# Block products in the second block's input projection, and a convolution split over three engines

## The reference

```python
u = h @ w_in_l                        # h: 512 x 1024, w_in_l: 1024 x 2048
ka, va = jnp.split(hc @ w_in_l[:, OFF_AK:OFF_BQ], 2, axis=-1)   # the 256 context tokens
...
def conformer_conv(u, conv_w, conv_b, ln_g, ln_b):
    a, gate = jnp.split(u, 2, axis=-1)
    h = a * jax.nn.sigmoid(gate)
    h = lax.conv_general_dilated(h, conv_w[:, None, :], window_strides=(1,), padding=((half, half),),
                                 feature_group_count=C_CHANNELS) + conv_b       # 31 taps, 256 channels
    return jax.nn.silu(layer_norm(h, ln_g, ln_b))
```

## Time and profile before

| what | value |
|---|---|
| median of 3 runs | 2835.19 us (2834.72 to 2843.73) |
| the profiled execution | 2836.13 us |
| span of its profile | 2834.3 us |
| mean granted clock of TensorE | 0.983 of full speed |
| `project2` in layer 0, first to last matmul | 974.85 to 1150.70 us |
| `project2` in layer 1 | 2004.33 to 2143.30 us |

### The profile page before, as it was taken

The page is one execution under the profiler, slowest core; times in us unless marked ns, Lnnn a source line. Parts: engine busy times, 40 slices in busy tenths (PEclk is TensorE's granted clock), DMA queues, the critical chain, the costliest instruction groups (busy, mean ns, idle before and its releaser), DMA issues. The chain is left out here.

```text
span 2834.3 us, 36392 instructions
## 1 busy us (share of the span) xinstructions
PE 2712.9 (96%) x15414; PEld 1568.9 (55%) x15414; DVE 1091.4 (39%) x2334; ACT 600.5 (21%) x1265; POOL 63.6 (2%) x61
## 2 busy tenths in 40 slices
PE   8998989999999999999799999999999989999998
PEld 7786755688864556764533333333777554444442
DVE  3523454477730365675620001113556560111212
ACT  4212234201110201562400000001215331001002
POOL 0000000000000000000001111110000000000000
PEclk9999999999999999999899999999999999999999
DMA  4228781222221211000489999996210038999995
GB/s 159 70 90 293 274 322 38 89 89 90 78 103 45 117 55 50 16 16 28 191 335 399 403 398 401 389 393 285 72 60 16 16 145 342 422 422 422 422 422 235
DMA packets 87478, 582.02 MB, mean 205 GB/s; under 512 B 10186, under 2 KB 11754, under 8 KB 21780
## 3 DMA queue, kind: packets, MB, share of 16 engines
q1 hardware_dynamic: 78244, 554.66, 49.3%
q0 software_dynamic: 6544, 21.24, 2.5%
q10 hardware_dynamic: 2528, 3.80, 0.4%
HBM read 561.96 MB, written 17.70 MB: 205 GB/s over the span
## 5 line engine op out<-in xcount | busy, mean ns | idle before, releaser
L3043 PE MATMUL ps<-ring,xsL 128*64 128x512 f32 x1320 | 298.2, 604 | 5.7 <-ACTq L217 5.7
L3043 PEld LDWEIGHTS ps<-ring,xsL 128*64 128x64 f32 x1320 | 96.2, 139 | 200.9 <-issue 194.9
L3301 DVE TENSOR_TENSOR hidL<-hidL,ps 128x1024 f32<-128x1024 f32 x16 | 19.5, 1221 | 473.6 <-PE ps L3043 473.6
L2618 PE MATMUL ps<-both,ring 128*128 128x384 f32 x480 | 158.0, 491 | 1.9 <-PEq L1834 1.9
L1841 PE MATMUL ps<-ring,actT 128*128 128x512 f32 x352 | 151.6, 592 | 1.1 <-PEq L2034 1.1
L3043 PE MATMUL ps<-ring,htL 128*64 128x512 f32 x640 | 143.9, 600 | 3.4 <-ACTq L217 3.2
L865 PE MATMUL ps<-both,ring 128*128 128x264 f32 x640 | 143.8, 386 | 1.4 <-PEq L642 1.4
L865 PEld LDWEIGHTS ps<-both,ring 128*128 128x128 f32 x640 | 121.4, 190 | 22.9 <-issue 2.3
L3331 ACT ACTIVATE hidL<-ps 128x1024 f32<-128x1024 f32 x16 | 16.4, 1024 | 541.7 <-PE ps L3051 303.4
L2618 PEld LDWEIGHTS ps<-both,ring 128*128 128x128 f32 x480 | 91.8, 192 | 66.5 <-issue 5.5
L2618 PE MATMUL ps<-tokens_b,ring 128*128 128x256 f32 (+1 forms) x480 | 121.9, 415 | 2.3 <-PEq L2223 2.3
(11 more groups left out here) (571 smaller groups left out, 3973.8 us busy)
## 6 DMA issues: line engine op xcount, KB each, us to landing
ring<-in_w_exp SPq DMA_DIRECT2D x245, 1024.0 KB, 13.7
ring<-in_w SPq DMA_DIRECT2D x73, 1024.0 KB, 5.0
tokens_b<-in_w_exp SPq DMA_DIRECT2D x63, 1024.0 KB, 13.8
ring<-in_w_mod SPq DMA_DIRECT2D x48, 1024.0 KB, 5.3
h<-in_w_exp SPq DMA_DIRECT2D x37, 1024.0 KB, 17.5
lent<-in_w_exp SPq DMA_DIRECT2D x26, 1024.0 KB, 15.9
both<-in_w_exp SPq DMA_DIRECT2D x13, 1024.0 KB, 18.6
gb<-in_rows SPq DMA_DIRECT2D x8, 512.0 KB
```

The lines of the kernel that those rows point to most:

```text
L2618: mm = pe.matmul(ps[:, bank + h, 0:half], w(c_), uT[:, c_, h * half:(h + 1) * half], start=c_ == 0, stop=c_ == KD - 1, skip_group_check=True)
L3043: mm = pe.matmul(ps[HD * par:HD * par + HD, bank + half, :], lhsL(kk, par), weights(kk)[:, half, par, :], start=kk == 0, stop=kk == KD - 1 ...
L3301: dve.tensor_tensor(h[:, :], h[:, :], src, ALU.mult).then_inc(hid.sem, 1)
```

## The change

Each chunk of weights becomes one 2 x 2 block product: the two halves of the input channels by the two tiles of columns on one side, by the two halves of the tokens on the other. It is made of seven block products in place of eight. A product has four matmuls of 128 x 128 weights by `H` tokens, 384 in layer 0 and 256 in layer 1. They go to four PSUM banks in the order P1, P7, P2 (on top of P1), P6, P5, P4, P3 (on top of P5). VectorE forms four sums of the token blocks once (`t1` to `t4`) and four sums of weight blocks per chunk (`s1` to `s4`), always for the next chunk, and combines the products in five sums per chunk. ScalarE copies P1 and later P1 + P2, and then scales or reorders the tiles (`finish_tiles`). In layer 1 the context's keys and values are made by plain products at the end of chunks KA, VB and KB (`context`). The values of the first attention come out with channels on the partitions like all others and are transposed afterwards (`turn_va`).

The convolution is split by group. Group 0 stays on VectorE, with its taps placed between the sums. For group 1 ScalarE writes each scaled, shifted tap into one of two buffers, and GpSimd adds it to `z`; `turn_z` waits for both groups. ScalarE takes over the copy of `vb` from VectorE, and the sums for the bias are split in two.

The eight sums need room: four of the ring's slots serve as scratch while `project2` runs. `slot_order` therefore gives the eight input chunks only four slots and puts the output projection's chunks into the scratch slots, and `limit` keeps their loads back until `project2` is over.

```diff
-            k.stream.limit = len(k.stream.chunks)
+            k.stream.limit = k.moe_at[0] - N_OUT2
...
+            stream.limit = k.moe_at[l + 1] - N_OUT2 if not last else len(stream.chunks)
...
+    K2, H = KD // 2, nq // 2
+    CIN, GATE, QA, QA2, KA, QB, VB, KB = range(N_IN2)
...
+    room_of = [k.stream.ring[:, x, :] for x in k.scratch[l]]
+    t1, t2, t3, t4 = (x[:, 0:K2 * H].rearrange("p (k t) -> p k t", k=K2) for x in room_of)
+    s1, s2, s3, s4 = (x[:, K2 * H:K2 * H + K2 * P].rearrange("p (k c) -> p k c", k=K2) for x in room_of)
+    b11, b12, b21, b22 = (uT[:, K2 * kh:K2 * kh + K2, h * H:(h + 1) * H] for kh in range(2) for h in range(2))
...
+            def product(out, w, x, start=True):
+                for c_ in range(K2):
+                    mm = pe.matmul(out, w[:, c_, :], x[:, c_, :], start=start and c_ == 0, stop=c_ == K2 - 1, skip_group_check=True)
+                mm.then_inc(ready.sem, 1)
...
+            def turn_va():
+                pe.wait_ge(assembled.sem, assembled.of(4 * KA + 3))
+                if kv:
+                    pe.wait_ge(ctx_read.sem, ctx_read.of(1))
+                for t in range(NT2):
+                    mm = pe.transpose(at_va[:, P * t:P * t + P], plain[1][:, P * t:P * t + P], c("ident"))
+                mm.then_inc(a_turned.sem, 1)
...
-                pe.wait_ge(filtered.sem, filtered.of(1))
+                pe.wait_ge(filtered.sem, filtered.of(2))
+                pe.wait_ge(a_taken.sem, a_taken.of(1))
...
-                project(i)
+            for i in range(N_IN2):
+                stream.wait(pe, chunk[i])
+                if i:
+                    pe.wait_ge(copied.sem, copied.of(2 * i))
+                product(bank(0), block_of(i, 0, 0), b11)
+                if i == QB:
+                    turn_va()
+                elif i == KB:
+                    rotate(3)
+                pe.wait_ge(weight_sums.sem, weight_sums.of(3 * i + 1))
+                if i:
+                    pe.wait_ge(assembled.sem, assembled.of(4 * i - 1))
+                product(bank(1), s3, t3)
+                pe.wait_ge(copied.sem, copied.of(2 * i + 1))
+                product(bank(0), block_of(i, 0, 1), b21, start=False)
+                if i == VB:
+                    turn_z()
+                pe.wait_ge(weight_sums.sem, weight_sums.of(3 * i + 2))
+                if i - 1 in kv:
+                    pe.wait_ge(ctx_read.sem, ctx_read.of(sum(x < i for x in kv)))
+                product(bank(2), s2, t2)
+                if i == VB:
+                    rotate(2)
+                elif i == KB:
+                    rotate(4)
+                    turn_values()
+                if i:
+                    pe.wait_ge(assembled.sem, assembled.of(4 * i))
+                product(bank(3), s1, t1)
+                if i == VB:
+                    turn_back()
+                pe.wait_ge(weight_sums.sem, weight_sums.of(3 * i + 3))
+                pe.wait_ge(assembled.sem, assembled.of(4 * i + 1))
+                product(bank(1), block_of(i, 1, 1), t4)
+                if i == QB:
+                    rotate(1)
+                pe.wait_ge(assembled.sem, assembled.of(4 * i + 2))
+                product(bank(3), s4, b22, start=False)
+                if i in kv:
+                    context(i)
+                stream.freed(chunk[i], ready.sem, ready.of(at(i, CONTEXT if i in kv else P4)))
...
+            def finish_tiles(i):
+                for j in (1, 0):
+                    act.wait_ge(assembled.sem, assembled.of(4 * i + 4 - j))
+                    x = tiles[i][j]
+                    if i == GATE:
+                        steps.free(act.activation(x[:, 0:nq], x[:, 0:nq], ACT.Sigmoid))
+                    elif i in (QA, QA2):
+                        steps.free(act.activation(x[:, 0:nq], x[:, 0:nq], ACT.Identity, scale=scale))
...
+            def scale_taps(first, after):
+                act.wait_ge(padded.sem, padded.of(1))
+                for tap in range(first, after):
+                    w, src = c2("conv_w", 2 * tap + 1), pad[:, 1, tap:tap + n_out]
+                    if tap >= 3:
+                        act.wait_ge(tap_added.sem, tap_added.of(tap - 2))
+                    if tap == 0:
+                        y = act.activation(z[:, 1, :], src, ACT.Identity, scale=w, bias=c2("conv_b", 1))
+                    else:
+                        y = act.activation(scaled_tap(tap), src, ACT.Identity, scale=w)
+                    y.then_inc(tapped.sem, 1)
+            for i in range(N_IN2):
+                act.wait_ge(ready.sem, ready.of(at(i, P1)))
+                if i == KB:
+                    act.wait_ge(filtered.sem, filtered.of(2))
+                act.copy(part(i, 0, 0), bank(0)).then_inc(copied.sem, 1)
...
+                if QA <= i <= VB:
+                    scale_taps(*((0, 4), (7, 10), (14, 17), (21, 24), (28, CW))[i - QA])
...
+                act.wait_ge(assembled.sem, assembled.of(4 * i + 1))
+                act.copy(part(i, 0, 0), bank(0)).then_inc(copied.sem, 1)
...
+                if QA <= i < VB:
+                    scale_taps(*((4, 6), (10, 13), (17, 20), (24, 27))[i - QA])
...
+                if i not in (CIN, KA):
+                    finish_tiles(i)
+                if QA <= i < VB:
+                    scale_taps(*((6, 7), (13, 14), (20, 21), (27, 28))[i - QA])
...
+            def first_sums(i):
+                dve.wait_ge(copied.sem, copied.of(2 * i + 1))
+                dve.wait_ge(ready.sem, ready.of(at(i, P6)))
+                steps(plus(part(i, 0, 1), bank(2), part(i, 0, 0)))
+                steps.free(plus(part(i, 1, 0), bank(1), part(i, 0, 1)))
+                steps.tell(assembled.sem)
+            def second_sum(i):
+                dve.wait_ge(ready.sem, ready.of(at(i, P5)))
+                steps.free(plus(part(i, 1, 1), bank(3), part(i, 1, 0)))
+                steps.tell(assembled.sem)
+                if i + 1 < N_IN2:
+                    stream.wait(dve, chunk[i + 1])
+                    steps.free(minus(s3, block_of(i + 1, 0, 0), block_of(i + 1, 1, 0)))
+                    steps.free(plus(s1, block_of(i + 1, 1, 0), block_of(i + 1, 1, 1)))
+                    steps.tell(weight_sums.sem)
+            def third_sum(i):
+                dve.wait_ge(ready.sem, ready.of(at(i, P4)))
+                steps.free(minus(part(i, 1, 0), part(i, 1, 0), bank(1)))
+                steps.tell(assembled.sem)
+                if i + 1 < N_IN2:
+                    steps.free(minus(s2, s1, block_of(i + 1, 0, 0)))
+                    steps.tell(weight_sums.sem)
+            def last_sum(i):
+                dve.wait_ge(ready.sem, ready.of(at(i, P3)))
+                steps.free(plus(part(i, 0, 1), bank(3), part(i, 0, 1)))
+                steps.tell(assembled.sem)
+                if i + 1 < N_IN2:
+                    steps.free(minus(s4, block_of(i + 1, 0, 1), s2))
+                    steps.tell(weight_sums.sem)
+            def convolve(first, after):
+                for tap in range(first, after):
+                    w, src = c2("conv_w", 2 * tap), pad[:, 0, tap:tap + n_out]
+                    if tap == 0:
+                        steps(dve.tensor_scalar(z[:, 0, :], src, w, c2("conv_b", 0), ALU.mult, ALU.add))
+                    else:
+                        steps(dve.scalar_tensor_tensor(z[:, 0, :], src, w, z[:, 0, :], ALU.mult, ALU.add))
...
+            stream.wait(dve, chunk[0])
+            steps.free(minus(t3, b22, b12))
+            steps.free(minus(s3, block_of(0, 0, 0), block_of(0, 1, 0)))
+            steps.tell(weight_sums.sem)
...
+            for i in (CIN, GATE):
+                first_sums(i)
+                second_sum(i)
+                third_sum(i)
+                last_sum(i)
...
+            steps.tell(padded.sem)
+            convolve(0, 4)
+            first_sums(QA)
+            convolve(4, 5)
+            second_sum(QA)
+            third_sum(QA)
+            convolve(5, 6)
+            last_sum(QA)
+            convolve(6, 13)
+            first_sums(QA2)
+            convolve(13, 14)
+            second_sum(QA2)
+            third_sum(QA2)
+            convolve(14, 15)
+            last_sum(QA2)
+            convolve(15, 22)
+            first_sums(KA)
+            convolve(22, 23)
+            second_sum(KA)
+            third_sum(KA)
+            convolve(23, 24)
+            last_sum(KA)
+            convolve(24, CW)
...
+            first_sums(QB)
+            second_sum(QB)
+            third_sum(QB)
...
+            first_sums(VB)
+            second_sum(VB)
+            rope(2)
+            third_sum(VB)
+            last_sum(VB)
+            rope(3)
+            first_sums(KB)
+            second_sum(KB)
...
+            add_bias(0, 2)
+            third_sum(KB)
+            rope(4)
+            add_bias(2, len(NEAR_PIECES))
+            last_sum(KB)
...
+        @block.gpsimd
+        def _(pool):
+            for tap in range(1, CW):
+                pool.wait_ge(tapped.sem, tapped.of(tap + 1))
```

(55 more changed lines are left out.)

165 lines of the change are left out of this document (83 added, 82 removed).

## The result

The changed kernel takes 2860.2 us, median of 5 runs (2856.0 to 2863.4), against 2835.2 for the kernel before (5 runs, 2832.1 to 2843.7); the ratio is 1.0087 with an interval of 1.0073 to 1.0101. It is slower, and above the forecast (2809) and the range (to 2846). The profiled execution took 2863.4 us, its span 2861.6.

The account below looks back on a forecast made before the run. TensorE, busy 2712.9 of 2834.3 us, was taken as the bound. Savings of 33.7 us, less 1.3, 4.2, 0.9 and 1.0, plus 0.6, gave 26.9 us and a forecast of 2809, range 2803 to 2846.

Parts of the forecast that it names:

- Seven adds per chunk are 11.2 us, under 18.1 and 12.1: hidden at either bound: In `project2`, GpSimd's adds at 1.6 us each fit within TensorE's chunk time in layers 0 and 1, costing nothing there.
- Rival one: GpSimd adds and VectorE instructions with two SBUF operands cannot run together: whole gain goes, about 2836 us; chance 0.35.
- TensorE's work: Block products in `project2` save TensorE 20.4 us in layer 0 and 13.3 in layer 1, together 33.7.
- VectorE: Taps and sums per chunk: 15.7 us against TensorE's 18.1 in layer 0, 12.5 against 12.1 in layer 1; 1 us charged.
- ScalarE: Copies, final scaling and taps per chunk take 9.8 of 18.1 us and 7.9 of 12.1: hidden, but taps wait for GpSimd.
- GpSimd's price: One convolution add takes 1.45 us plus 0.15 to hand over in both layers; lower bound 0.98 and 0.69.
- `turn_z`: After the last convolution adds, TensorE waits 1.2 us in layer 0 and 3.0 in layer 1, 4.2 together.
- Small stalls: Waits in `project2`: 1.3 us at the start, 0.9 at the return after `turn_z`, 1.0 for VectorE in layer 1.
- Transfers: Output projection loads moved to the mixers, and input chunks 4 to 7 loaded three chunks ahead, cost nothing.
- Tail: At the last keys, one more sum costs 0.2 us in layer 0; context products save 0.8 in layer 1.
- Rival one's formula: Excess 30a - 35 us in layer 0, 30a - 25 in layer 1, a being an add's length; 27 us at 1.45.

## Why the prediction was wrong

The step that failed is "Seven adds per chunk are 11.2 us, under 18.1 and 12.1: hidden at either bound". It compares GpSimd's chain with TensorE's chunk alone. The additions took VectorE's time as well: the 30 taps took 49.0 and 31.5 us for 31.0 and 22.6 without additions, and VectorE had only some 2.4 us to spare per chunk in layer 0 and none in layer 1, by the prediction's own sums. TensorE then waited for VectorE. In all the additions cost 47 us, some 14 of them also without VectorE's taps. Rival one said that they would shut each other out and had 0.35 against 0.42.

Term by term:
- **TensorE's work**: right in layer 0, 2.1 us short in layer 1. Without the additions TensorE is busy for 155.9 and 127.8 us, 19.9 and 11.2 less than in the earlier trace rows, against 20.4 and 13.3 predicted.
- **VectorE**: right as long as nothing contends. Taps are 1.03 and 0.75, and nine taps and a chunk's sums fit (the kernel without additions).
- **ScalarE**: a tap took 0.95 and 0.72 us (estimate 1.0 and 0.8). Its queue was warned of, and cost two waits in layer 1, 1.62 and 0.71 us.
- **GpSimd's price**: 1.45 was too low at 783 columns (median 1.84 alone) and too high at 512 (1.27). The upper bound of the range, 1.45, was no bound: it came from an instruction of another kind. The prediction's estimate of 1.7 and 1.1 from the Trainium skill's figure, on the page "GPSIMD Engine Reference", section "Elementwise — side-by-side cycle accounting", was nearer to these rows.
- **`turn_z`**: 2.71 and 4.07 us measured, 1.2 and 3.0 predicted. GpSimd's last additions are what it waits for, as forecast.
- **Small stalls** (start 1.3, return 0.9, VectorE in layer 1 1.0): over-priced as waits. Without additions TensorE idles 0.3 and 1.5 us in all.
- **Transfers**: right, no wait of TensorE for a load of the output projection is in the trace.
- **Tail**: mis-sized. 0.2 us was charged in layer 0; the mixers wait 4.30 us where they waited 1.54, and 4.30 without additions too. Four bias subtractions (1.96 us) stand ahead of the last sum in VectorE's queue; with the sum ahead of them the wait was 3.40, and the subtractions ended last. In layer 1 the wait fell from 1.54 to 1.22 us, 0.3 saved of the 0.8 charged.
- **Rival one's formula**: with means of 1.80 and 1.36 us for an addition beside no taps (53.9 and 40.9 us for 30) it gives 30 x 1.80 - 35 + 30 x 1.36 - 25 = 35 us, so 2844. What is missing is the clock, which the prediction named as a danger and did not price: 9.6 + 7.1 = 16.8 us, half as much again. 2809 + 35 + 17 is 2861 against 2860 measured; some of that closeness is luck, since the forecast without additions was itself 4 us low (2809 against 2813).

## What to carry to other kernels

Work handed to GpSimd is not free beside VectorE: count the time of GpSimd's instructions that read SBUF together with VectorE's instructions that read two SBUF operands as one engine's, and ask whether that sum fits the stage. Where it does not, put VectorE's running operand in PSUM, which cost the taps nothing here (though two rotations had to move to free the bank), before giving up the split. A chain of short waits on TensorE costs more than the waits: here half as much again through the clock.

## What the runs showed of the hardware

- VectorE and GpSimd took turns instruction by instruction, 2.39 us for a pair of one tap (1.03 alone) and one addition (median 1.84 alone), so a pair is 0.5 us shorter than the two after each other.
- GpSimd's two-operand addition took 1.57 to 1.84 us at 783 columns and 1.26 at 512, its copy 1.18 and 0.78 on average, its memset 0.75 and 0.53; a tap on VectorE cost the same with its sum in PSUM (1.038) as in SBUF (1.034).
- After TensorE had idled for 4.64 or 6.35 us its next product ran at the 1.2 GHz level (5.46 us for 2.74); after 3.55 us once at full speed (2.82), in layer 1 after 3.86 us at 3.29 and 3.75 for 1.89. In two other versions a product took 4.51 us after a wait of only 1.97 (the whole convolution on VectorE) and 2.00 (sums in PSUM, changed order). What decides between the two is not settled by these runs.
